# Latent attention: k-v product, turning of v and the next head's maxima one step later in the order of the queues

## Chip, cores and metric

One core of a Trainium2 chip. The metric is the device time of one execution in microseconds (us), lower is better.

## The reference, cut to what matters

The kernel computes two transformer blocks on 1024 positions. The change touches one stage of the second block, the latent attention (mla_mixer) with 12 heads. For each head:

```
q  = (rms_norm(c_q)  @ w_q_up)    # 96 columns: 64 plain, 32 turned by the positions (rope)
kv = (rms_norm(c_kv) @ w_kv_up)   # 64 columns of k, 64 of v; k gets the 32 shared rope columns
s  = q . k * 96**-0.5, causal mask; p = softmax(s); out = p @ v
```

All of it is float32 work to nearly full precision: every factor is held as a high part (fp32r) and a low part (the rest), and a product is three matmuls, high by high, high by low and low by high.

## The kernel before, in words

The five engines have queues of their own, written out as Python loops under `@block.tensor` (PE), `@block.scalar` (ACT), `@block.vector` (DVE), `@block.gpsimd` (POOL, which splits weight slabs into high and low parts) and `@block.sync` (SP, which loads them). They are held together by semaphores alone: `wait_ge` stands in the queue, and what is behind it on that engine waits too.

The latent attention runs in steps, one for each tile of transposed scores, keys by queries. A head has two chunks of 512 queries and in each the key blocks of 128 that the mask leaves: `HEAD_TILES`, 4 tiles in chunk 0 and 8 in chunk 1, so `N_HT` = 12 steps, called 0 to 11 here. The last four tiles of each chunk lie on the diagonal; they are 512, 384, 256 and 128 queries wide. For tile u:

- PE `scores(u)` (L870 the three products, L872 a fourth that subtracts each query's maximum by means of a diagonal matrix `dg`, L875 the mask on the diagonal). It goes into one of the two buffers `aux`. The first tile of chunk c waits for `dg_ready` of maximum 4c + 3, the last of its chunk.
- ACT `exponential(u)` (L1374, px) and `high_part(u)` (L1380, px_h); DVE `low_part(u)` (L1488, px_l).
- PE `values(u)` (L888, L889, L891), which stands `AV_LAG` = 2 steps later.
- Three steps after a chunk's last tile, ACT takes the logarithm of the row sums (L1391) and turns it into the inverse (L1397), around that step's `high_part`, and DVE multiplies (L1946, `weighted`).

A head needs beforehand the maxima of its queries, 8 blocks of 128: `maximum(h, i)` on PE (L852, L854) makes plain scores of block i against (i + 1) x 128 keys into the one buffer `ps[:, 0]`, DVE reduces them (L1922, which frees the buffer by `mx_free`) and writes the diagonal matrix (`diagonal`, L1929). They run `MAX_LEAD` = 5 steps ahead of the head's own steps: maxima 0 to 4 in steps 7 to 11 of the head before, 5 to 7 in steps 0 to 2.

And the next head's q, k and v are made meanwhile, in the one buffer `ps[:, 1]`: PE `latent_q` in steps 0, 1 and 2 (L811, from cq), `latent_kv` in step 4 (L811, from ckv), `latent_vt` in step 6 (the turning of v, eight transposes of kvf, L840). The ways out of the buffer stand in a table `parts` by step, behind the step's other work. ACT: 3 q without rope, 4 high part of q (qa_h), 5 the copy kvf, 6 high part of k (ka_h), 7 high part of v. DVE: 3 the rope product (L1902, qf), 5, 7 and 8 the low parts of q, k and v (L1488). `latent_kv` waits for both q parts of step 3 to have left the buffer, `latent_vt` for kvf, `maximum(h + 1, 0)` for qa_h and ka_h.

The order within a step is, on PE: scores, maximum, latent piece, values; on DVE: maximum and diagonal, low part, part, weighted; on ACT: exponential, logarithm, high part, inverse, part. The loops are quoted in the listing and the diff:

Of the kernel before, what the change touches and what calls it, by code (L numbers as in the profile page):

```python
# [35 lines left out]
MLA_HEADS = 12  # L36
# [53 lines left out]
def program(nc, wall, vecs, consts, xt, pt, memt, pos, spill_x, spill_o, spill_out, spill_gate, out):  # L90
# [240 lines left out]
             ({}, 4)  # L331
    HEAD_TILES = [(c, kb, max(kb * P - c * HALF, 0)) for c in range(2) for kb in range(4 * c + 4)]
    N_HT = len(HEAD_TILES)
    AV_LAG, MAX_LEAD = 2, 5

    def maximum_of(step):

        h, i = divmod(step + MAX_LEAD, N_HT)
        return (h, i) if i < 8 else (None, None)
# [55 lines left out]
    def _(pe):  # L395
# [34 lines left out]
        def product(ks, rh, rl, n=S, ready=None, sl=None):  # L430
            sl = slab() if sl is None else sl
            w, slot = work()
            proj(slot, sl, ks, rh, rl, n, ready)
            return w
# [37 lines left out]
        def norm_row(n):  # L472

            pe.wait_ge(rs_ready, t.next(rs_ready))
            for j in range(n // P):
                m = pe.transpose(row[:, j * P:(j + 1) * P], rs[:, j:j + 1].broadcast_to([P, P]), ident)
            m.then_inc(row_done, 1)
# [5 lines left out]
        def with_sums(make):  # L483

            for m in range(KT):
                make(m)
            tile_sums(KT, S)
# [134 lines left out]
        def from_split(ktiles):  # L622
            base = t.take(tile_split, ktiles)
            return lambda i: pe.wait_ge(tile_split, base + i + 1)
# [157 lines left out]
        def output():  # L782
            ready = from_split(KT)
            with_sums(lambda m: product(range(KT), y_h, y_l, ready=ready if m == 0 else None))
            norm_row(S)
# [32 lines left out]
        def latent_q(h, k):  # L818
            if k == 0:
                if h > 0:  # L820
                    pe.wait_ge(vl_ready, h)
                state["slab"] = slab()
            if h == 0:
                readyq(k)
            m = latent_product(state["slab"], [k], 0, 2, cq_h, cq_l, 0)
            if k == 2:
                m.then_inc(q_done, 1)

        def latent_kv(h):
            pe.wait_ge(qn_ready, h + 1)  # L830
            pe.wait_ge(rope_ready, h + 1)
            if h == 0:
                for i in range(2):
                    readykv(i)
            latent_product(state["slab"], [3, 4], 3, 4, ckv_h, ckv_l, 3).then_inc(kv_done, 1)

        def latent_vt(h):
            pe.wait_ge(kvf_ready, h + 1)
            for k in range(KT):
                m = pe.transpose(ps[:, 1, k * P:(k + 1) * P], kvf[:, k * P:(k + 1) * P], ident)  # L840
            m.then_inc(vt_done, 1)

        def maximum(h, i):

            n, keys = 8 * h + i, (i + 1) * P
            if n > 0:
                pe.wait_ge(mx_free, n)
            if i == 0:
                pe.wait_ge(qh_ready, h + 1)
                pe.wait_ge(kh_ready, h + 1)  # L850
            for a, b in widths(keys):
                pe.matmul(ps[:, 0, a:b], qa[h % 2][0][:, i * P:(i + 1) * P], ka[h % 2][0][:, a:b],  # L852
                          start=True, stop=(b < keys), skip_group_check=True)
            pe.matmul(ps[:, 0, keys - P:keys], id_r[:, :], neg_q, start=False, stop=True,  # L854
                      skip_group_check=True).then_inc(mx_done, 1)

        def scores(u):
            h, i = divmod(u, N_HT)
            c, kb, n0 = HEAD_TILES[i]
            if u >= 2:  # L860
                pe.wait_ge(ph_ready, u - 1)
            if i == 0:
                pe.wait_ge(ql_ready, h + 1)
                pe.wait_ge(kl_ready, h + 1)
            if kb == 0:
                pe.wait_ge(dg_ready, 8 * h + 4 * c + 4)
            q, k = qa[h % 2], ka[h % 2]
            st = aux[:, u % 2, n0:HALF]
            for j, (kp, qp) in enumerate(((0, 0), (0, 1), (1, 0))):
                pe.matmul(st, k[kp][:, kb * P:(kb + 1) * P], q[qp][:, c * HALF + n0:(c + 1) * HALF],  # L870
                          start=(j == 0), stop=False, skip_group_check=True)
            m = pe.matmul(st, ones_r[:, :], dg[:, c, n0:HALF], start=False, stop=(kb < 4 * c),  # L872
                          skip_group_check=True)
            if kb >= 4 * c:
                m = pe.matmul(aux[:, u % 2, n0:n0 + P], neg_q, id_r[:, :], start=False, stop=True, skip_group_check=True)  # L875
            m.then_inc(st_done, 1)

        def values(u):
            h, i = divmod(u, N_HT)
            c, kb, n0 = HEAD_TILES[i]  # L880
            g, last = 2 * h + c, kb == 4 * c + 3
            if i == 0:
                pe.wait_ge(vl_ready, h + 1)
            if kb == 0 and g >= 2:
                pe.wait_ge(ot_made, g - 1)
            pe.wait_ge(ph_ready, u + 1)
            ph, pl = px_h[u % 4][:, n0:HALF], px_l[u % 4][:, n0:HALF]
            pe.matmul(ob[:, g % 2, n0:HALF], v1[h % 2][:, kb, :], ph, start=(kb == 0), stop=False, skip_group_check=True)  # L888
            pe.matmul(ob[0:64, g % 2, n0:HALF], vl[h % 2][:, kb, :], ph, start=False, stop=False, skip_group_check=True)  # L889
            pe.wait_ge(pl_ready, u + 1)  # L890
            pe.matmul(ob[:, g % 2, n0:HALF], v1[h % 2][:, kb, :], pl, start=False, stop=last,  # L891
                      skip_group_check=True).then_inc(at_done, 1)
# [7 lines left out]
        for step in range(MLA_HEADS * N_HT + AV_LAG):  # L900
            h, i = divmod(step, N_HT)
            if h < MLA_HEADS:
                scores(step)
            mh, mi = maximum_of(step)
            if mh is not None and mh < MLA_HEADS:
                maximum(mh, mi)
            if h + 1 < MLA_HEADS:
                if i < 3:
                    latent_q(h + 1, i)
                elif i == 4:  # L910
                    latent_kv(h + 1)
                elif i == 6:
                    latent_vt(h + 1)
            if step >= AV_LAG:
                values(step - AV_LAG)
        output()


# [27 lines left out]
    def _(act):  # L946
# [417 lines left out]
            act.wait_ge(vt_done, h + 1)  # L1364
            copy(v1[h % 2][:, :, 0:64], ps[:, 1, :].rearrange("p (k f) -> p k f", k=8)[:, :, 64:P]).then_inc(vh_ready, 1)

        parts = {3: latent_q_nope, 4: latent_q_high, 5: latent_kv, 6: latent_k_high, 7: latent_v_high}

        def exponential(u):
            n0 = HEAD_TILES[u % N_HT][2]  # L1370
# [34 lines left out]
        for step in range(n_tiles + 7):  # L1405
            h, i = divmod(step, N_HT)
# [57 lines left out]
    def _(dve):  # L1464
# [137 lines left out]
        for step in range(NU + 4):  # L1602
# [12 lines left out]
            if 0 <= m < NU:  # L1615
# [4 lines left out]
                i = dve.scalar_tensor_tensor(out=e[:, :, 0:n], in0=z[:, :, 0:n], scalar=0.0, in1=e[:, :, 0:n],  # L1620
                                             op0=ALU.max, op1=ALU.add)
                if kb >= 4 * chunk:
# [3 lines left out]
                    i = dve.tensor_tensor(e[:, :, 0:c1], e[:, :, 0:c1], mask, ALU.mult)  # L1626
# [67 lines left out]
        def low_part(k):  # L1694
            dve.wait_ge(nh_ready, t.next(nh_ready))
            dve.scalar_tensor_tensor(out=hl[:, k, :], in0=x_t[:, k, :], scalar=vcol(V_MLP + k),
                                     in1=hh[:, k, :].bitcast(F32), op0=ALU.mult, op1=ALU.subtract).then_inc(norm_ready, 1)
# [216 lines left out]
            low(vl[h % 2][:, :, :], ps[:, 1, :].rearrange("p (k f) -> p k f", k=8)[:, :, 64:P],  # L1914
                v1[h % 2][:, :, 0:64]).then_inc(vl_ready, 1)

        parts = {3: latent_rope, 5: latent_q_low, 7: latent_k_low, 8: latent_v_low}

        def maximum(h, i):
            n = 8 * h + i  # L1920
            dve.wait_ge(mx_done, n + 1)
            dve.tensor_reduce(nm[:, n % 4:n % 4 + 1], ps[:, 0, 0:(i + 1) * P], AX.X, ALU.max, negate=True).then_inc(mx_free, 1)  # L1922

        def diagonal(h, i):
            n = 8 * h + i
            dve.wait_ge(mx_free, n + 1)
            if i % 4 == 0 and h > 0:
                dve.wait_ge(st_done, N_HT * h - (8 if i == 0 else 0))
            dve.tensor_scalar(dg[:, i // 4, i % 4 * P:(i % 4 + 1) * P], ident, nm[:, n % 4:n % 4 + 1],  # L1929
                              None, ALU.mult).then_inc(dg_ready, 1)  # L1930
# [24 lines left out]
        for step in range(n_tiles + AV_LAG + 2):  # L1955
            h, i = divmod(step, N_HT)
            mh, mi = maximum_of(step)
            if mh is not None and mh < MLA_HEADS:
                maximum(mh, mi)
            if mh is not None and mh < MLA_HEADS:  # L1960
                diagonal(mh, mi)
            if step < n_tiles:
                low_part(step)
            if h + 1 < MLA_HEADS and i in parts:
                parts[i](h + 1)
            done = step - AV_LAG - 1
            if done >= 0 and HEAD_TILES[done % N_HT][1] == 4 * HEAD_TILES[done % N_HT][0] + 3:
                weighted(done)
# [170 lines left out]
```

## Time and profile before

| what | before |
|---|---|
| median of 3 runs | 3587.58 us (3586.64 to 3592.84) |
| the profiled execution | 3589.34 us |
| its span | 3587.5 us |
| mean granted clock of PE over the span | 0.953 |
| busy: PE, DVE, ACT, POOL | 88%, 51%, 31%, 30% |
| latent attention in the span | about 2216 to 2568 us |

All times of rows are microseconds from the start of the span. PE stands for the matmuls, PEld for the loads of their weights beside them. Matmuls are pipelined and their ends are modelled, so a row's duration is longer than its distance to the next row. In a timeline, brackets show the idle time before a row and who ended it.

### The profile page before, as it was taken

The page shows a single profiled execution, that of the slowest core. Times are in us where ns is not written, and L with a number is a line of the kernel's source. Part 1 is how long each engine was busy: PE and PEld are TensorE (multiplying, and loading weights), DVE is VectorE, ACT ScalarE, POOL GpSimd, SP SyncE. Part 2 cuts the span into 40 slices and gives each one's busy share as a digit, 9 for nine tenths or more (in the row PEclk, how much of TensorE's full clock was granted, in tenths as well). Part 3 has the DMA queues.
Part 4 walks back from the last instruction along what each step waited for, and adds up shares of the span by engine and source line. Part 5 has one row for each costly group of instructions (what it writes and reads, how often), then busy time and mean ns, then how long its engine had stood idle before and what let it go on. Part 6 is the DMA issues. An engine that isn't in the chain of part 4 may idle for free.

```text
span 3587.5 us, 37646 instructions
## 1 busy us (share of the span) xinstructions
PE 3167.1 (88%) x15158; PEld 2616.9 (73%) x15158; DVE 1837.2 (51%) x2041; ACT 1104.9 (31%) x1682; POOL 1093.1 (30%) x426
## 2 busy tenths in 40 slices
PE   5888799999999999999787987999795789999897
PEld 4666578887788888887676776777574677777786
DVE  5788842112324334445665345777627556666543
ACT  2666720001220001001322223555523333333411
POOL 2111034444434444444245322111141211111152
PEclk9999999999899999999788998999896999999998
DMA  2000021112111111111122112000211000000131
GB/s 92 18 30 24 18 94 47 49 51 88 42 36 48 53 47 47 47 53 53 36 88 59 53 58 87 24 30 24 118 42 59 30 24 24 24 24 24 49 116 65
DMA packets 44572, 179.03 MB, mean 50 GB/s; under 512 B 4672, under 2 KB 5696, under 8 KB 43392
## 3 DMA queue, kind: packets, MB, share of 16 engines
q1 hardware_dynamic: 32976, 119.88, 11.0%
q10 hardware_dynamic: 11440, 56.89, 4.0%
q8 instruction: 120, 1.97, 0.2%
q14 instruction: 36, 0.29, 0.0%
HBM read 147.39 MB, written 29.36 MB: 49 GB/s over the span
## 4 chain that ended last, share of the span: by engine, by line
PE 75%; DVE 12%; ACT 7%; issue 4%; POOL 1%; DMA 1%; ACTq 0%; DVEq 0%; SPq 0%; POOLq 0%
PE ps L423 55%; PE ps L707 3%; PE ps L811 2%; PE ob L449 2%; PE ob L742 2%; PE aux L870 2%; PE ps L523 1%; ACT pt_h L966 1%; PE aux L725 1%; DVE pt_l L1488 1%; ACT prob L1214 1%; DVE zb L1608 1%; DVE acc L1513 1%; PE ps L852 1%; PE aux L552 1%
## 5 line engine op out<-in xcount | busy, mean ns | idle before, releaser
L380 POOL TENSOR_TENSOR wh<-raw,con 128x1024 fp32r<-128x1024 f32 x211 | 512.8, 2430 | 2433.6 <-PE ps L423 1902.7
L423 PE MATMUL ps<-hh,wh 128*128 128x512 f32 x1984 | 625.3, 397 | 39.8 <-DVE hl L1488 22.8
L423 PE MATMUL ps<-hl,wh 128*128 128x512 f32 x1984 | 619.9, 394 | 0.0
L423 PE MATMUL ps<-hh,wl 128*128 128x512 f32 x1984 | 618.4, 393 | 0.0
L382 POOL TENSOR_TENSOR wl<-raw,wh 128x1024 fp32r<-128x1024 f32 x211 | 580.2, 2750 | 16.6
L423 PEld LDWEIGHTS ps<-hh,wh 128*128 128x128 f32 x1984 | 373.6, 191 | 126.5 <-issue 36.3
L423 PEld LDWEIGHTS ps<-hl,wh 128*128 128x128 f32 x1984 | 378.5, 191 | 80.2
L423 PEld LDWEIGHTS ps<-hh,wl 128*128 128x128 f32 x1984 | 377.6, 190 | 80.2
L1730 DVE TENSOR_TENSOR y_t<-y_t,ps 128x1024 f32<-128x1024 f32 x120 | 146.5, 1221 | 174.5 <-PE ps L423 174.5
L1137 ACT ACTIVATE ff<-fr 128x1024 f32<-128x1024 f32 x32 | 34.0, 1061 | 563.7 <-DVE fr L1719 563.7
L1775 DVE TENSOR_REDUCE small<-ps 128x1 f32<-128x256 f32 (+3 forms) x160 | 105.7, 660 | 146.7 <-PE ps L707 85.1
L423 PE MATMUL ps<-f_h,wh 128*128 128x512 f32 x512 | 158.3, 390 | 2.7 <-DVE f_l L1488 2.5
L423 PE MATMUL ps<-f_h,wl 128*128 128x512 f32 x512 | 158.4, 391 | 0.0
L423 PE MATMUL ps<-f_l,wh 128*128 128x512 f32 x512 | 158.1, 390 | 0.0
L1488 DVE TENSOR_TENSOR pt_l<-aux,pt_h 128x512 fp32r<-128x512 f32 x152 | 104.4, 690 | 87.8 <-ACT pt_h L966 85.2
L1783 DVE TENSOR_SCALAR prob<-prob,small 128x256 f32<-128x256 f32 (+3 forms) x160 | 143.2, 895 | 5.7
L1513 DVE TENSOR_TENSOR acc<-acc,sq 128x1024 f32<-128x1024 f32 x40 | 80.1, 2002 | 123.9 <-ACT sq L979 123.5
L1719 DVE SCALAR_TENSOR_TENSOR fr<-ps,row_sb 128x1024 f32<-128x1024 f32 x32 | 39.2, 1224 | 192.1 <-PE ps L423 192.1
L1214 ACT ACTIVATE prob<-ps,small 128x256 f32<-128x256 f32 (+3 forms) x160 | 106.5, 665 | 46.9 <-DVE small L1775 45.7
L966 ACT ACTIVATE pt_h<-aux 128x512 fp32r<-128x512 f32 x152 | 90.3, 597 | 98.7 <-PE aux L725 97.5
L1374 ACT ACTIVATE px<-aux 128x512 f32<-128x512 f32 (+2 forms) x144 | 70.8, 492 | 155.4 <-PE aux L875 120.5
L1488 DVE TENSOR_TENSOR px_l<-px,px_h 128x512 fp32r<-128x512 f32 (+2 forms) x144 | 79.7, 553 | 71.8 <-ACT px_h L1380 71.8
(322 smaller groups left out, 5990.2 us busy)
## 6 DMA issues: line engine op xcount, KB each, us to landing
raw<-wall SPq DMA_DIRECT2D x211, 512.0 KB, 3.6
spill_x<-x_t ACTq DMA_DIRECT2D x2, 4096.0 KB, 12.1
spill_out<-ot ACTq DMA_DIRECT2D x16, 512.0 KB, 2.6
go<-spill_out ACTq DMA_DIRECT2D x16, 512.0 KB, 4.3
xold_t<-spill_x ACTq DMA_DIRECT2D x2, 4096.0 KB, 15.5
x_t<-xt SPq DMA_DIRECT2D x8, 512.0 KB, 8.9
spill_o<-op ACTq DMA_DIRECT2D x4, 1024.0 KB, 3.9
o_all<-spill_o ACTq DMA_DIRECT2D x2, 2048.0 KB, 10.3
```

Of the source, the lines that this page charges most:

```text
L380: pool.tensor_tensor(wh[:, s, :, :], raw[:, s, :, :], ones.unsqueeze(1).broadcast_to([P, KT, P]), ALU.mult).then_inc(w_high, 1)
L382: pool.tensor_tensor(wl[:, s, :, :], raw[:, s, :, :], wh[:, s, :, :].bitcast(F32), ALU.subtract).then_inc(w_split, 1)
L423: m = pe.matmul(ps[:, w, a:b], lw[:, sl, k, :], r[:, i, a:b], start=(i == 0 and j == 0), stop=(i == len(ks) - 1 and j == 2))
L449: m = pe.matmul(ob[:, bank, j:j + 1], src[:, j * P:(j + 1) * P], ones[:, 0:1], start=False, stop=True, skip_group_check=True)
L707: m = pe.matmul(ps[:, slot, a:b], l, r[0:n_rows, a:b], start=(j == 0), stop=(j == len(parts) - 1 and not masked), skip_group_check=True)
L966: return act.activation(out_, in_, ACT.Copy, scale=scale)
L1214: act.activation(prob[now % 2][i][:, 0:keys], ps[:, w % 2, 0:keys], ACT.Exp, bias=nm[:, j:j + 1], scale=1.0, accum_out=rsum[:, j:j + 1]).t ...
L1488: return dve.tensor_tensor(dst, src, hi.bitcast(F32), ALU.subtract)
L1513: dve.tensor_tensor(acc[:, :], acc[:, :], sq[(first + k) % 2][:, :], ALU.add).then_inc(sq_used, 1)
L1730: dve.tensor_tensor(y_t[:, m, :], y_t[:, m, :], ps[:, slot, :], ALU.add).then_inc(work_free[slot], 1)
L1775: dve.tensor_reduce(nm[:, i:i + 1], ps[:, slot, 0:keys_of(n % 4)], AX.X, ALU.max, negate=True).then_inc(nm_ready, 1)
L1783: dve.tensor_scalar(p, p, rinv[:, i:i + 1], None, ALU.mult).then_inc(pn_ready, 1)
```

## The change

The lead of the maxima falls from 5 steps to 4: maxima 0 to 3 in steps 8 to 11, 4 to 7 in steps 0 to 3. On PE the k-v product moves from step 4 to 5 and the turning of v from 6 to 7; maximum 0 stands behind the values of its step. On ACT the parts of k and v (kvf, ka_h, high part of v) each move one step, on DVE the low parts of k and v; there maximum 0 and its diagonal stand behind the low part of the step. The q parts stay.

```
--- before.py
+++ after.py
@@ -331,7 +331,7 @@
              ({}, 4)
     HEAD_TILES = [(c, kb, max(kb * P - c * HALF, 0)) for c in range(2) for kb in range(4 * c + 4)]
     N_HT = len(HEAD_TILES)
-    AV_LAG, MAX_LEAD = 2, 5
+    AV_LAG, MAX_LEAD = 2, 4
 
     def maximum_of(step):
 
@@ -902,17 +902,20 @@
             if h < MLA_HEADS:
                 scores(step)
             mh, mi = maximum_of(step)
-            if mh is not None and mh < MLA_HEADS:
+            due = mh is not None and mh < MLA_HEADS
+            if due and mi > 0:
                 maximum(mh, mi)
             if h + 1 < MLA_HEADS:
                 if i < 3:
                     latent_q(h + 1, i)
-                elif i == 4:
+                elif i == 5:
                     latent_kv(h + 1)
-                elif i == 6:
+                elif i == 7:
                     latent_vt(h + 1)
             if step >= AV_LAG:
                 values(step - AV_LAG)
+            if due and mi == 0:
+                maximum(mh, mi)
         output()
 
 
@@ -1364,7 +1367,7 @@
             act.wait_ge(vt_done, h + 1)
             copy(v1[h % 2][:, :, 0:64], ps[:, 1, :].rearrange("p (k f) -> p k f", k=8)[:, :, 64:P]).then_inc(vh_ready, 1)
 
-        parts = {3: latent_q_nope, 4: latent_q_high, 5: latent_kv, 6: latent_k_high, 7: latent_v_high}
+        parts = {3: latent_q_nope, 4: latent_q_high, 6: latent_kv, 7: latent_k_high, 8: latent_v_high}
 
         def exponential(u):
             n0 = HEAD_TILES[u % N_HT][2]
@@ -1914,7 +1917,7 @@
             low(vl[h % 2][:, :, :], ps[:, 1, :].rearrange("p (k f) -> p k f", k=8)[:, :, 64:P],
                 v1[h % 2][:, :, 0:64]).then_inc(vl_ready, 1)
 
-        parts = {3: latent_rope, 5: latent_q_low, 7: latent_k_low, 8: latent_v_low}
+        parts = {3: latent_rope, 5: latent_q_low, 8: latent_k_low, 9: latent_v_low}
 
         def maximum(h, i):
             n = 8 * h + i
@@ -1955,12 +1958,15 @@
         for step in range(n_tiles + AV_LAG + 2):
             h, i = divmod(step, N_HT)
             mh, mi = maximum_of(step)
-            if mh is not None and mh < MLA_HEADS:
+            due = mh is not None and mh < MLA_HEADS
+            if due and mi > 0:
                 maximum(mh, mi)
-            if mh is not None and mh < MLA_HEADS:
                 diagonal(mh, mi)
             if step < n_tiles:
                 low_part(step)
+            if due and mi == 0:
+                maximum(mh, mi)
+                diagonal(mh, mi)
             if h + 1 < MLA_HEADS and i in parts:
                 parts[i](h + 1)
             done = step - AV_LAG - 1
```

## Rows read from the trace of the kernel before

**Rows 1.** Busy time in two stretches: stick-breaking stage, ten heads of latent attention. Columns: first line.

```profile
core 0: us, PE busy (x) PEld busy (x) DVE busy (x) ACT busy (x) POOL busy (x), PEclk, DMA share, GB/s
80.00:470.00 390.00, 316.74 (x1445) 243.49 (x1444) 311.77 (x331) 258.14 (x319) 47.73 (x18) 0.95 0.07 22
2228.32:2529.03 300.71, 277.48 (x1500) 229.91 (x1501) 218.94 (x340) 170.91 (x331) 52.64 (x20) 1.00 0.08 25
```

**Rows 2.** The waits between 2228 and 2559 us: us in total, times, longest.

```profile
PE ps L840 <- ACT kvf L966: 9.8, 11, 0.9
PE ps L811 <- DVE qf L1902: 7.9, 11, 0.7
PE ps L852 <- ACT ka_h L966: 7.6, 11, 0.8
```

**Rows 3.** Timeline of PE over one head: start, duration, operation, idle before.

```profile
2324.78 1.09 PE L840 MATMUL ps<-con,kvf 128*128 128x128 f32 x8 [0.90 <-ACT kvf L966]
2325.63 0.48 PE L888 MATMUL ob<-px_h,v_b 128*128 128x512 f32 x1
...
2326.88 0.39 PE L870 MATMUL aux<-qa_h,ka_l 128*128 128x512 f32 x1
2327.10 0.40 PE L872 MATMUL aux<-dg,ones_r 128*128 128x512 f32 x1
2328.34 0.30 PE L852 MATMUL ps<-ka_h,qa_h 128*128 128x128 f32 x1 [0.84 <-ACT ka_h L966]
...
2328.59 0.44 PE L888 MATMUL ob<-px_h,v_b 128*128 128x512 f32 x1
...
2330.32 0.33 PE L852 MATMUL ps<-ka_h,qa_h 128*128 128x256 f32 x1
...
2335.24 0.51 PE L852 MATMUL ps<-ka_h,qa_h 128*128 128x512 f32 x2
...
2335.69 0.39 PE L888 MATMUL ob<-px_h,v_b 128*128 128x384 f32 x1
...
2336.26 0.40 PE L870 MATMUL aux<-qa_h,ka_h 128*128 128x512 f32 x1
...
2348.63 0.70 PE L811 MATMUL ps<-ckv_h,wh 128*128 128x512 f32 x2 [0.72 <-DVE qf L1902]
```

**Rows 4.** Timelines of PE, then DVE, in the last head, from maximum 7.

```profile
2551.17 0.73 PE L852 MATMUL ps<-ka_h,qa_h 128*128 128x512 f32 x2 [0.31 <-DVE small L1922]
...
2551.79 0.45 PE L888 MATMUL ob<-px_h,v_b 128*128 128x512 f32 x1
...
2553.68 0.47 PE L870 MATMUL aux<-qa_h,ka_h 128*128 128x512 f32 x1
...
2553.25 0.29 DVE L1929 TENSOR_SCALAR dg<-con,small 128x128 fp32r<-128x128 f32 x1
```

**Rows 5.** Timeline of ACT over the same head, steps 5, 6 and 8.

```profile
2323.70 1.03 ACT L966 ACTIVATE kvf<-ps 128x1024 f32<-128x1024 f32 x1
2324.61 0.62 ACT L1374 ACTIVATE px<-aux 128x512 f32<-128x512 f32 x1
...
2327.14 1.06 ACT L966 ACTIVATE ka_h<-kvf 64x1024 fp32r<-64x1024 f32 x1
...
2330.51 0.60 ACT L1374 ACTIVATE px<-aux 128x512 f32<-128x512 f32 x1 [0.87 <-PE aux L875]
2331.01 0.59 ACT L1380 ACTIVATE px_h<-aux 128x512 fp32r<-128x512 f32 x1
```

**Rows 6.** Timeline of DVE over the same head, reduction 0 to diagonal 3.

```profile
2328.79 0.29 DVE L1922 TENSOR_REDUCE small<-ps 128x1 f32<-128x128 f32 x1 [0.88 <-PE ps L854]
...
2329.32 0.69 DVE L1488 TENSOR_TENSOR px_l<-px,px_h 128x512 fp32r<-128x512 f32 x1
2329.92 1.21 DVE L1488 TENSOR_TENSOR ka_l<-kvf,ka_h 64x1024 fp32r<-64x1024 f32 x1
...
2334.90 0.29 DVE L1929 TENSOR_SCALAR dg<-con,small 128x128 fp32r<-128x128 f32 x1
2335.10 0.42 DVE L1488 TENSOR_TENSOR px_l<-px,px_h 128x256 fp32r<-128x256 f32 x1
```

More of the change, by code:

```diff
@@ L333, in program @@
     N_HT = len(HEAD_TILES)
-    AV_LAG, MAX_LEAD = 2, 5
+    AV_LAG, MAX_LEAD = 2, 4
     def maximum_of(step):
@@ L904, in _ @@
             mh, mi = maximum_of(step)
-            if mh is not None and mh < MLA_HEADS:
+            due = mh is not None and mh < MLA_HEADS
+            if due and mi > 0:
                 maximum(mh, mi)
@@ L909, in _ @@
                     latent_q(h + 1, i)
-                elif i == 4:
+                elif i == 5:
                     latent_kv(h + 1)
-                elif i == 6:
+                elif i == 7:
                     latent_vt(h + 1)
@@ L915, in _ @@
                 values(step - AV_LAG)
+            if due and mi == 0:
+                maximum(mh, mi)
         output()
@@ L1365, in latent_v_high @@
             copy(v1[h % 2][:, :, 0:64], ps[:, 1, :].rearrange("p (k f) -> p k f", k=8)[:, :, 64:P]).then_inc(vh_ready, 1)
-        parts = {3: latent_q_nope, 4: latent_q_high, 5: latent_kv, 6: latent_k_high, 7: latent_v_high}
+        parts = {3: latent_q_nope, 4: latent_q_high, 6: latent_kv, 7: latent_k_high, 8: latent_v_high}
         def exponential(u):
@@ L1915, in latent_v_low @@
                 v1[h % 2][:, :, 0:64]).then_inc(vl_ready, 1)
-        parts = {3: latent_rope, 5: latent_q_low, 7: latent_k_low, 8: latent_v_low}
+        parts = {3: latent_rope, 5: latent_q_low, 8: latent_k_low, 9: latent_v_low}
         def maximum(h, i):
@@ L1957, in _ @@
             mh, mi = maximum_of(step)
-            if mh is not None and mh < MLA_HEADS:
+            due = mh is not None and mh < MLA_HEADS
+            if due and mi > 0:
                 maximum(mh, mi)
-            if mh is not None and mh < MLA_HEADS:
                 diagonal(mh, mi)
@@ L1963, in _ @@
                 low_part(step)
+            if due and mi == 0:
+                maximum(mh, mi)
+                diagonal(mh, mi)
             if h + 1 < MLA_HEADS and i in parts:
```

## Prediction

> **What bounds the kernel now.** I read the page for the shares, then the busy time by stretches, then the waits of the stage that the diff touches, and last the timelines of PE, ACT and DVE over one head. In the ten full heads of the latent attention, 2228.32 to 2529.03 us, the granted clock is 1.00, the level of 2.4 GHz, and PE is busy 277.48 of 300.71 us, 27.8 of 30.07 per head; the other engines have room [rows 1]. So the stage goes by PE's own queue, and what can be won or lost is PE's standing still. The reader should look in the waits for lines that name PE: only three come once per head, 11 times each, for the k-v product (ps<-ckv, L811, waits for qf), the turning of v (L840, waits for kvf) and the next head's first maximum (L852, waits for ka_h) [rows 2]. The change moves just these three.
>
> I number the steps 0 to 11 within a head. A 512-column matmul of the scores is shown 0.40 long, while the next starts 0.23 after it, at 2327.10 behind 2326.88 [rows 3]. A shown idle time must therefore be enlarged by about 0.16 to get the time in which PE issued nothing. The three waits are then 0.72 + 0.16 = 0.88, 0.90 + 0.16 = 1.06 and 0.84 + 0.16 = 1.00, together **2.94 us per head** [rows 3]; all three gone would be 32 us.
>
> **The change part by part.** No instruction and no DMA is added or removed; the order in the queues of PE, ACT and DVE is. SP and POOL keep their code: the weight slab of the next head is asked for by the same q product in step 0. What POOL does to DVE's diagonals while it splits the slab now falls on maxima 4 and 5, not 5 and 6; only the low parts of steps 0 and 1 stand behind them, and PE wants those two steps later. I cost it at nothing.
>
> *k-v product, step 4 to 5.* It waits for the q copy on ACT and the rope product on DVE, both of part 3. It gets the PE work of scores 5 and values 2 in between, over a microsecond, and the wait of 0.88 goes. Late next are the scores of step 4 themselves (next point).
>
> *Maxima 1 to 7, one step later.* The last maximum (1024 keys) was in step 2, a whole step ahead of the scores of step 4, which need its diagonal (dg_ready). It now stands in step 3, with only values 1 behind it. The last head shows the round trip without other work: the maximum's matmuls start at 2551.17, the scores of step 4 at 2553.68, so 2.51 us through the reduction, the diagonal and back [rows 4]. PE's own work in that time will be the maximum (2551.17 to 2551.79, 0.62) and values 1 (0.57, as for the 384 columns of values 9, 2335.69 to 2336.26 [rows 3]). **New wait at scores 4: 2.51 - 0.62 - 0.57 = 1.32 us.** Bounds 1.1 and 1.5. Rope now stands behind that last reduction on DVE (and behind the low part of step 3), but it ends before PE is through scores 4, values 2 and scores 5.
>
> *Turning of v, step 6 to 7.* It needs the copy kvf on ACT, which moves from ACT's step 5 to step 6. There ACT's queue holds the two exponentials of the tile and, because chunk 0 ended three steps before, the logarithm and the inverse of its sums, all ahead of the moved part. Before, ka_h stood in that place: from px at 2324.61 to ka_h at 2327.14 are 2.53 us [rows 5]. kvf now starts 2.53 us after px of step 6, lasts 1.03, and the turning follows 0.05 later (2323.70 + 1.03 against 2324.78) [rows 3, 5]. px starts 0.19 after PE has issued its scores (2330.32 and 2330.51) [rows 3, 5]. PE covers values 4 and scores 7, 2325.63 to 2327.10 and 0.23 more, 1.70 us [rows 3]. **Wait at the turning: 0.19 + 2.53 + 1.03 + 0.05 - 1.70 = 2.10 us**, in place of 1.06. In the heads where ACT's pair is a little shorter it is 0.25 less, and so was the old wait for ka_h; the balance is the same. Bounds 1.8 and 2.4.
>
> *First maximum, step 7 to the end of step 8.* It needs ka_h, which ACT now makes in step 7, right behind kvf and two exponentials; meanwhile PE turns v and does values 5, scores 8 and values 6, some 3 us. The old wait of 1.00 goes. But on DVE its reduction now stands behind low part 8, which waits for px_h of the same step, and all maxima share one buffer, so each waits for the reduction before (mx_free). DVE has been nearly without a gap from reduction 0 to diagonal 3: 2328.79 to 2334.90 + 0.29, 6.40 us [rows 6]. That chain keeps k_low, v_low, the four reductions and diagonals, loses low parts 7 and 8 (0.60 each, 2329.32 to 2329.92) and takes low part 10 (0.42 long, some 0.35 in sequence) in place of nothing: 6.40 - 1.20 + 0.35 = 5.55 us [rows 6]. It starts, counted from the end of scores 8 on PE, after 0.19 to px, 0.50 to px_h, 0.59 of px_h, 0.04, and low part 8 (0.60): 1.92 [rows 5, 6]. The last diagonal ends at 7.47, and the next head's scores 0, which need it, start 0.14 later (as from 2553.25 + 0.29 to 2553.68): 7.61 [rows 4]. PE's own work in that time was 2330.32 to 2336.26, 5.94; it loses maximum 4 (2335.24 to 2335.69, 0.45) and gets maximum 0 (0.25, 2328.34 to 2328.59): 5.74 [rows 3]. **Waits of maxima 1 to 3 and of scores 0 together: 7.61 - 5.74 = 1.87 us per head.** By my split they are 0.5, 0.3, 0.3 and 0.8. Bounds 0.9 (only the wait of scores 0, which no order of the low parts hides) and 2.5 (each handover dearer by 0.15).
>
> *Ends of the stage.* In the last head no q product parts the maxima 4 to 7, and DVE is already late there (0.31 idle before the last maximum [rows 4]); I take 1.9 us for it, between 1.3 (the wait of scores 4 alone) and 2.5. Before the first head one maximum of 640 keys leaves the serial prologue: 0.45 at full clock [rows 3], twice that at the half level; I take -0.5, between 0 and -1.0.
>
> **Sum.** Per head 1.32 + 2.10 + 1.87 - 2.94 = +2.35 us, over 11 heads +25.9; with +1.9 and -0.5 it is **+27.3 us**. The profiled execution took 3589.34 us with a span of 3587.5, the median is 3587.58; I put the sum on the median: **3614.9 us**, 0.76% slower. What a measurement of this kernel can tell from no change is about 0.2%, 7 us.
>
> **Rivals.** *DVE keeps pace.* If the waits of 1.87 did not arise, because DVE's chain packs more tightly than its rows show, +0.48 per head remains: 5.3 + 1.3 - 0.5 = +6 us, 3593.7, just inside no change. For it: the six rows of the chain are read out of a queue that was itself waiting now and then. Against it: the reduction of maximum 0 comes behind low part 8 by the code, and scores 0 need a diagonal whose maximum stands one short values group ahead. Chance 0.08.
>
> *The clock falls.* PE's busy share would go from 0.92 to about 0.86. The stick-breaking stage from 80 to 470 us shows 316.74 of 390, 0.81, at a mean granted clock of 0.95, while this stage has 1.00 [rows 1]. If this stage fell to 0.95 as well, part of it at 1.2 instead of 2.4 GHz, its PE work of some 333 us (12 heads of 27.8 at most) would take 18 us more: +45, 3633. Against it: the longest new pause is 2 us, and the work round it is dense. Chance 0.04. The Trainium skill (TensorE: Matmul & The Clock Gate, section "HAM oscillation — how this bites in real kernels") tells of this mechanism: pauses between bursts of matmuls that throw the clock back to half again and again. By that rule the added pauses could cost more than their own length; the trace of before, with three pauses a head, shows no fall.
>
> *Faster.* The three old waits are real and each moved part has a step more. If kvf came through ACT ahead of the logarithm and the inverse, and DVE gave its diagonals in time, only the turning's wait would stay: -(0.88 + 1.00) x 11 = -21 us, 3567. The place is ACT's step 6, and the point is whether kvf starts within 1.49 us of px: then the turning waits 0.19 + 1.49 + 1.03 + 0.05 - 1.70 = 1.06, no longer than before. 2.53 us of work stand ahead of it in a queue that goes in order. Chance 0.03. That the change leaves the order as it was is ruled out by the code; that gains and losses cancel otherwise has 0.01.
>
> **How the numbers follow.** Forecast 0.84, DVE keeps pace 0.08, clock 0.04, faster 0.03, cancelled 0.01. With all terms at their low bounds a head costs 1.1 + 1.8 + 0.9 - 2.94 = +0.9, in all about +10; at their high ones 1.5 + 2.4 + 2.5 - 2.94 = +3.5, in all +40. These do not come all together, so the range is 3601 to 3627 us. Slower by over 0.2%: forecast, clock and a quarter of the second case, 0.90. Within 0.2%: 0.07. Faster: 0.03.
>
> **What would show it.** In the changed profile PE should be idle before L870 at step 4 with DVE small or dg named (about 1.2), before L840 with kvf (near 1.9), no longer before L811 and no longer for ka_h before L852; before L852 of maxima 1 to 3 some tenths for DVE small, before L870 of step 0 about 0.7. The head's period should go from 30.1 to 32.4 us. A period at or under 30.1, a wait at L840 of 1 us or less, or a granted clock under 1.00 would prove me wrong.

## The result, and the profile after

| what | before | after |
|---|---|---|
| median | 3590.21 us of 4 runs (3586.64 to 3594.32) | 3621.13 us of 4 runs (3618.60 to 3624.94) |
| ratio, with its 95% interval | | 1.0087 [1.0069, 1.0104] |
| span of the profiled execution | 3587.5 us | 3621.2 us |
| a head of the latent attention, mean of ten | 30.07 us | 32.54 us |

The change makes the kernel slower by 0.87%, 31 us by the medians of the same round; the forecast was 27 us and 0.76%. The same work is done: 37646 instructions in both. Busy times by stretch for ten heads, from k-v product to k-v product (columns: window, its length, then the busy time of each engine, the granted clock, DMA):

```profile
core 0: us, PE busy (x) PEld busy (x) DVE busy (x) ACT busy (x) POOL busy (x), PEclk, DMA share, GB/s
2233.41:2558.77 325.36, 283.55 (x1502) 231.97 (x1501) 222.08 (x340) 171.44 (x331) 52.65 (x20) 1.00 0.08 23
```

Against [rows 1], ten heads take 325.36 us in place of 300.71, with the same number of DVE and ACT instructions (340, 331) and the same granted clock of 1.00. PE's busy time is 6 us larger although it does the same work: the modelled end of a matmul covers the first 0.16 us of every pause, and there are now six pauses a head instead of three, which makes 4.8 of the 6 us. So the loss is standing time on PE. The waits of the stage name it (us in total, times, longest):

```profile
PEld ps L840 <- ACT kvf L969: 25.2, 11, 2.4
...
PE aux L870 <- DVE dg L1932: 20.9, 23, 1.4
PE ps L840 <- ACT kvf L969: 20.6, 11, 2.0
...
PE ps L852 <- DVE small L1925: 4.4, 12, 0.4
```

Compare [rows 2]. The waits of L811 for qf and of L852 for ka_h, 7.9 and 7.6 us, are gone. L840's wait for kvf is doubled, from 9.8 to 20.6, and L870's wait for a diagonal is new, 20.9 us in 23 pieces: twice in each of eleven heads (scores 4, and scores 0 of the next head), once in the last. The timeline of PE over one head shows where (it answers to [rows 3]):

```profile
2361.28 0.47 PE L870 MATMUL aux<-qa_h,ka_h 128*128 128x512 f32 x1 [1.15 <-DVE dg L1932]
...
2363.56 0.62 PE L811 MATMUL ps<-ckv_h,wh 128*128 128x512 f32 x2
...
2368.88 0.39 PE L872 MATMUL aux<-dg,ones_r 128*128 128x512 f32 x1
2371.01 1.09 PE L840 MATMUL ps<-con,kvf 128*128 128x128 f32 x8 [1.74 <-ACT kvf L969]
...
2375.89 0.39 PE L852 MATMUL ps<-ka_h,qa_h 128*128 128x256 f32 x1 [0.37 <-DVE small L1925]
...
2377.40 0.22 PE L875 MATMUL aux<-id_r,neg_r 128*128 128x128 f32 x1
2377.68 0.44 PE L852 MATMUL ps<-ka_h,qa_h 128*128 128x384 f32 x1
...
2379.15 0.27 PE L875 MATMUL aux<-id_r,neg_r 128*128 128x128 f32 x1
2379.53 0.50 PE L852 MATMUL ps<-ka_h,qa_h 128*128 128x512 f32 x1
...
2381.28 0.47 PE L870 MATMUL aux<-qa_h,ka_h 128*128 128x512 f32 x1 [0.62 <-DVE dg L1932]
...
2393.69 0.47 PE L870 MATMUL aux<-qa_h,ka_h 128*128 128x512 f32 x1 [1.15 <-DVE dg L1932]
```

The first row is the scores of step 4, the last row those of the next head. The pauses, with the modelled tails (0.16 to 0.17) added to what the brackets show, are 1.32 at scores 4, none at the k-v product, 1.90 at the turning, 0.53, 0.22 and 0.32 at maxima 1, 2 and 3, and 0.78 at scores 0. The short ones at maxima 2 and 3 carry no bracket, since the tail of the matmul before covers them: they are read off as 2377.40 + 0.06 against 2377.68 and 2379.15 + 0.06 against 2379.53. The heads come in two kinds that take turns, even and odd numbers from 0: this one is even (number 4), the head read before the change in [rows 3] is odd (number 3). In the odd heads the turning waits 2.18.

And the timeline of ACT in steps 6 and 7 of this head (it answers to [rows 5]):

```profile
2367.70 0.60 ACT L1377 ACTIVATE px<-aux 128x512 f32<-128x512 f32 x1 [2.08 <-PE aux L872]
2368.32 0.60 ACT L1394 ACTIVATE inv<-ob 64x512 f32<-64x512 f32 x1
2368.95 0.60 ACT L1383 ACTIVATE px_h<-aux 128x512 fp32r<-128x512 f32 x1
2369.44 0.62 ACT L1400 ACTIVATE inv<-inv 64x512 f32<-64x512 f32 x1
2369.96 1.00 ACT L969 ACTIVATE kvf<-ps 128x1024 f32<-128x1024 f32 x1
```

ACT stands idle for 2.08 us, although the k-v product it has to copy was there by 2366.5, because its queue wants the scores of step 6 first; then four softmax operations precede the copy. From px to kvf are 2.26 us here; in the odd head that follows they are 2.52 (2400.09 to 2402.61), which is the difference in the turning's wait. Why the two kinds differ was not looked into.

The timeline of DVE from low part 8 on (it answers to [rows 6]):

```profile
2374.95 0.69 DVE L1491 TENSOR_TENSOR px_l<-px,px_h 128x512 fp32r<-128x512 f32 x1 [2.30 <-ACT px_h L1383]
2375.56 0.28 DVE L1925 TENSOR_REDUCE small<-ps 128x1 f32<-128x128 f32 x1
...
2376.08 1.21 DVE L1491 TENSOR_TENSOR ka_l<-kvf,ka_h 64x1024 fp32r<-64x1024 f32 x1
...
2378.32 0.68 DVE L1491 TENSOR_TENSOR vl_b<-ps,v_b 128x512 fp32r<-128x512 f32 x1
...
2380.12 0.69 DVE L1925 TENSOR_REDUCE small<-ps 128x1 f32<-128x512 f32 x1
2380.85 0.29 DVE L1932 TENSOR_SCALAR dg<-con,small 128x128 fp32r<-128x128 f32 x1
```

From reduction 0 to the end of diagonal 3 DVE is never idle for 5.58 us, and the scores that need the diagonal start 0.14 later, at 2381.28.

### The profile page after: what moved, and what is told of

Read it like the earlier page. It is cut to its first block, busy times and chain, and to the rows that moved or that the text cites. A ratio compares the mean times of both kernels' runs of the same rounds, so it can differ in the third digit from the quotient of the medians.

```text
span 3621.2 us, 37646 instructions
## 1 busy us (share of the span) xinstructions
PE 3188.7 (88%) x15158; PEld 2631.3 (73%) x15158; DVE 1841.2 (51%) x2041; ACT 1105.1 (31%) x1682; POOL 1093.4 (30%) x426
## 4 chain that ended last, share of the span: by engine, by line
PE 74%; DVE 14%; ACT 7%; issue 4%; POOL 1%; DMA 1%; ACTq 0%; DVEq 0%; SPq 0%; POOLq 0%
PE ps L423 54%; PE ps L707 3%; PE ps L811 2%; PE ob L449 2%; PE aux L870 2%; PE ob L742 2%; ACT pt_h L969 1%; PE aux L725 1%; PE ps L523 1%; DVE pt_l L1491 1%; ACT prob L1217 1%; DVE small L1925 1%; PE aux L552 1%; DVE zb L1611 1%; DVE acc L1516 1%
## 5 line engine op out<-in xcount | busy, mean ns | idle before, releaser
L1140 ACT ACTIVATE ff<-fr 128x1024 f32<-128x1024 f32 x32 | 33.9, 1061 | 563.7 <-DVE fr L1722 563.7
```

## The experiments

Each kernel was timed against the kernel before. "Head" is the mean distance of the k-v products over ten heads of its profile, "stage" the time from the first scores to the last values product, which is free of what the rest of the program does from run to run (the part ahead of the stage alone differed by 3.2 us between the first two profiles).

| kernel | ratio to before [95%] | head, us | stage, us |
|---|---|---|---|
| before | 1 | 30.07 | 350.78 |
| the change | 1.0087 [1.0069, 1.0104] | 32.54 | 380.05 |
| e1, lead alone | 1.0057 [1.0040, 1.0074] | 31.70 | 372.47 |
| e2, pieces alone | 1.0019 [1.0008, 1.0030] | 30.69 | 357.18 |
| e3, change, copy first on ACT | 1.0020 [1.0009, 1.0032] | 30.65 | 359.24 |
| e4, change, maximum 7 first | 1.0080 [1.0063, 1.0097] | 32.56 | 379.77 |
| e5, change, low part of v later | 1.0070 [1.0051, 1.0088] | 32.40 | 378.46 |
| e6, the three waits gone | 0.9917 [0.9903, 0.9931] | 27.44 | 321.98 |
| e8, e6 with DVE as before | 0.9941 [0.9925, 0.9958] | 28.51 | 333.62 |
| e9, e6 with lead 4 | 0.9990 [0.9980, 0.9999] | 29.53 | 348.75 |

**Lead alone.** The kernel before, with

```
-    AV_LAG, MAX_LEAD = 2, 5
+    AV_LAG, MAX_LEAD = 2, 4
```

> The maxima alone one step later (lead 4), k-v product and turning as before. Theory (each wait is the chain on DVE or ACT less PE's cover): scores of step 4 wait 1.32 us for the last diagonal; the k-v product, still in step 4, waits some 0.5 for rope, which now stands behind that reduction; the turning 1.06 as before; the first maximum no more; scores 0 some 0.8. In all 3.7 against 2.94 us a head, so 11 x 0.8, plus 1.9 in the last head, less 0.6 before the first: about +10 us against before, head period 30.9. Rival (the whole loss of the change is the shorter lead of the maxima, and the moved pieces are a gain by themselves): +31 us or more.

It came out twice as dear, +20 us of the medians and +21.7 in the stage. The waits in two heads of the profile: 1.32 at scores 4, 0.46 at the k-v product, 1.06 at the turning and 0.79 at scores 0, all as expected, and besides 0.53 or 0.26 at maximum 1 and 0.29 at maximum 2, which I had put at nothing. DVE's timeline shows why:

```profile
2339.14 1.21 DVE L1488 TENSOR_TENSOR ka_l<-kvf,ka_h 64x1024 fp32r<-64x1024 f32 x1
2340.28 0.28 DVE L1922 TENSOR_REDUCE small<-ps 128x1 f32<-128x128 f32 x1
2340.59 0.29 DVE L1929 TENSOR_SCALAR dg<-con,small 128x128 fp32r<-128x128 f32 x1
2340.79 0.68 DVE L1488 TENSOR_TENSOR px_l<-px,px_h 128x512 fp32r<-128x512 f32 x1
2341.39 0.69 DVE L1488 TENSOR_TENSOR vl_a<-ps,v_a 128x512 fp32r<-128x512 f32 x1
2341.99 0.42 DVE L1922 TENSOR_REDUCE small<-ps 128x1 f32<-128x256 f32 x1
```

The low part of k (step 7) stands ahead of reduction 0, that of v (step 8) ahead of reduction 1, and PE needs the single maxima buffer back sooner than they let DVE come to it. I had also taken 2.94 us a head as the old wait; the mean of both kinds of head is 2.81. And some 1.5 us of the 21.7 are no price of the lead: the last head took 22.8 us against 21.3 in the changed kernel, since PE's clock fell behind the pause before scores 4. The first row below is the matmul that ends the pause, the second the stretch behind it (columns as in [rows 1], granted clock 0.50):

```profile
2576.62 0.51 PE L870 MATMUL aux<-qa_h,ka_h 128*128 128x512 f32 x1 [1.44 <-DVE dg L1929]
2576.90:2580.30 3.40, 3.40 (x11) 2.79 (x10) 0.69 (x1) 1.09 (x2) 0.00 (x0) 0.50 0.00 0
```

The rival, that the lead is the whole loss, falls: it is two thirds of it.

**Pieces alone.** The changed kernel, with

```
-    AV_LAG, MAX_LEAD = 2, 4
+    AV_LAG, MAX_LEAD = 2, 5
```

> The k-v product, the turning of v and their ways out one step later, maximum 0 last in its step 7, but the lead of the maxima stays 5. Theory: no wait at the k-v product and none of scores 4 or scores 0 for a diagonal; the turning waits 1.9 for kvf as in the changed kernel, since the copy stands behind the logarithm and the inverse on ACT; maximum 0 waits 0.4 for ka_h, maxima 3 and 4 about 0.4 each for DVE. Some 3.1 against 2.94 us a head: +2 us against before (between -3 and +8). Rival (moved pieces are a gain): the turning waits 1.06 or less and the kernel is 10 to 21 us faster than before.

+6.2 us by the medians, +6.4 in the stage. The turning waits 1.90 or 2.18, maximum 0 0.37 or 0.53, maxima 3 and 4 0.36 and 0.39; the rival is refuted. Two of ten heads took 31.7 us instead of 30.7, since PE's clock fell behind the pause at the turning. In one of them the pause lasted until 2331.31 (busy times of three stretches, the granted clock is the third figure from the end):

```profile
2325.00:2331.30 6.30, 4.29 (x21) 3.18 (x19) 3.21 (x4) 3.98 (x8) 0.00 (x0) 1.00 0.00 0
2331.30:2335.50 4.20, 4.19 (x17) 3.67 (x18) 1.27 (x3) 1.99 (x3) 0.00 (x0) 0.59 0.00 0
2335.50:2340.00 4.50, 4.31 (x26) 3.72 (x25) 3.60 (x7) 3.11 (x7) 0.00 (x0) 1.00 0.00 0
```

Most of that middle stretch was granted 1.2 GHz, the rest 2.4. Of the 0.62 us that a head costs more than before, these two falls make 0.2 in the mean of ten, and the waits the rest.

**Copy first.** The changed kernel, on ACT (the part of step 6 is left out of the table's call):

```
             done = step - AV_LAG - 1
+            if i == 6 and h + 1 < MLA_HEADS:
+                latent_kv(h + 1)
             if step < n_tiles:
                 exponential(step)
```

> The changed kernel with one thing moved: on ACT the copy kvf comes first in step 6, ahead of the exponential, where ACT stands idle for 2.1 us. Theory (the turning's wait of 1.90 is the order of ACT's queue): the wait at L840 is gone, the other waits stay, -1.9 x 11 = -21 us against the changed kernel, +10 against before, head period 30.5. Rival (ACT as a whole is late, or the waits merely move on to DVE's chain, which must run anyway): less than 5 us are won and the waits of maxima 1 to 3 and of scores 0 grow by what the turning loses.

23 us below the changed kernel by the two medians (25 if each is taken against the kernel before of its own rounds), 20.8 in the stage, as the theory said (21). ACT's and PE's timelines of one head:

```profile
2362.03 1.03 ACT L969 ACTIVATE kvf<-ps 128x1024 f32<-128x1024 f32 x1 [0.88 <-PE ps L811]
2363.24 0.60 ACT L1377 ACTIVATE px<-aux 128x512 f32<-128x512 f32 x1 [0.19 <-PE aux L872]
```

```profile
2364.43 0.39 PE L872 MATMUL aux<-dg,ones_r 128*128 128x512 f32 x1
2364.66 1.03 PE L840 MATMUL ps<-con,kvf 128*128 128x128 f32 x8
```

The copy fits into ACT's idle time and is over before the scores of step 6 are; the turning follows the scores of step 7 without a bracket. The other waits stayed (1.32, 0.53 or 0.73, 0.22, 0.32, 0.79). So the turning's wait was the order of ACT's queue: with one copy moved it is gone, and of the other waits only those of maxima 0 and 1 grew, by 0.14 and 0.2 in every other head.

**Maximum 7 first.** The changed kernel, on PE:

```
+            if due and mi == 7:
+                maximum(mh, mi)
             if h < MLA_HEADS:
                 scores(step)
-            if due and mi > 0:
+            if due and 0 < mi < 7:
                 maximum(mh, mi)
```

> The changed kernel with one thing moved on PE: maximum 7 stands ahead of the scores of step 3 instead of behind them. Theory (the wait of scores 4, 1.32 us, is the fixed way through reduction and diagonal less the work that PE has in between): 0.50 us of scores are added to the cover, the wait falls to 0.8 in the full heads, less in the last one where DVE is late; -5 to -6 us against the changed kernel, +25 against before. Rival (the wait ends when DVE is through its queue, however early the maximum comes): the wait stays 1.3 and the time too.

The time as a whole did not move by more than its noise, but the head did, in both directions. Where nothing else happened it took 31.86 and 32.29 us, against 32.40 and 32.67: the wait of scores 4 fell from 1.32 to 0.95, not quite to 0.82. DVE's timeline has the missing 0.13:

```profile
2350.81 1.95 DVE L1934 TENSOR_SCALAR dg<-con,small 128x128 fp32r<-128x128 f32 x1
...
2354.26 1.44 DVE L1934 TENSOR_SCALAR dg<-con,small 128x128 fp32r<-128x128 f32 x1
...
2357.86 0.69 DVE L1951 TENSOR_TENSOR ot<-ob,inv 64x512 f32<-64x512 f32 x1
2358.57 1.23 DVE L1927 TENSOR_REDUCE small<-ps 128x1 f32<-128x1024 f32 x1
```

DVE is never idle from diagonal 4 to reduction 7, which starts 0.44 us behind the maximum's last matmul (2358.13), where in the changed kernel it starts 0.26 behind it (0.05 of the 0.18 comes back, since the maximum's own matmuls are shorter by that). Two diagonals in that chain, 4 and 5, took 1.95 and 1.44 us instead of 0.29; they lie beside POOL's splitting of the next weight slab (2350.28 to 2355.62). Three heads took 33.9 us, each with its clock falling behind the turning's pause, 1.6 us more than its like: 4.9 us, as much as the shorter wait wins (11 times some 0.45). For the wait the theory holds for 0.37 us of the 0.50, and the rival, DVE's queue, for the rest; the total is inconclusive.

**Low part of v later.** The changed kernel, on DVE:

```
-        parts = {3: latent_rope, 5: latent_q_low, 8: latent_k_low, 9: latent_v_low}
+        parts = {3: latent_rope, 5: latent_q_low, 8: latent_k_low, 11: latent_v_low}
```

> The changed kernel with the low part of v moved on DVE from step 9 to step 11, behind the last diagonal that scores 0 need. Theory (the waits of maxima 1 to 3 and of scores 0, 1.85 us together, are one chain on DVE that has no gap): the chain is 0.60 us shorter and so are the waits, to 1.25; -6.6 us against the changed kernel, +25 against before. Rival (each of these waits is the latency of one handover between PE and DVE, whatever else DVE does): they stay 0.5, 0.2, 0.3 and 0.8 and the time stays.

Half of what the theory said: a head of 32.11 or 32.38 us, 0.3 less, with one head of 34.0 where the clock fell (the medians, 3618.88 against 3621.13, are too close to tell). The wait of maximum 3 is gone, those of maxima 1 and 2 stay (DVE's work ahead of them is the same), and that of scores 0 stays at 0.78. DVE's timeline tells why the last did not follow:

```profile
2383.24 0.42 DVE L1491 TENSOR_TENSOR px_l<-px,px_h 128x256 fp32r<-128x256 f32 x1
2383.93 0.69 DVE L1925 TENSOR_REDUCE small<-ps 128x1 f32<-128x512 f32 x1 [0.27 <-PE ps L854]
2384.66 0.29 DVE L1932 TENSOR_SCALAR dg<-con,small 128x128 fp32r<-128x128 f32 x1
```

Once DVE is early enough, reduction 3 waits for PE's maximum, and the way from there through reduction, diagonal and back is fixed. In the changed kernel both limits lay in the same place: there reduction 3 starts at 2380.12, without a bracket, right behind the low part of its step.

**The three waits gone.** The kernel before, with the k-v product in step 5 on PE, and

```
# ACT
+            ahead = i == 6 and h + 1 < MLA_HEADS
+            if ahead:
+                latent_kv(h + 1)
             if step < n_tiles:
                 exponential(step)
+            if ahead:
+                latent_k_high(h + 1)
...
# DVE
-        parts = {3: latent_rope, 5: latent_q_low, 7: latent_k_low, 8: latent_v_low}
+        parts = {3: latent_rope, 5: latent_q_low, 10: latent_v_low}
...
+            if i == 6 and h + 1 < MLA_HEADS:
+                latent_k_low(h + 1)
             if step < n_tiles:
                 low_part(step)
```

> The kernel before, with the k-v product in step 5, the turning still in step 6, the lead still 5; on ACT kvf first in step 6 and ka_h right behind that step's first exponential; on DVE the low part of k ahead of low part 6 and the low part of v in step 10. Theory (the three waits of before, 2.94 us a head by the one head read and some 2.8 in the mean, are orders of queues and not work): they fall to some 0.1 to 0.4 a head, -27 to -31 us against before, head period 27.4, about 3560 us. Rival (DVE's chain of reductions, diagonals and low parts is the bound behind them, 6.4 us without a gap): the waits come back at L852 for DVE small, and less than 15 us are won.

3561.30 us against 3591.96, 30.7 us faster than before, ratio 0.9917 [0.9903, 0.9931], a head of 27.44 us. The rows show first two waits of DVE and ACT that cost nothing, since both have idle time there, and then all that is left of PE's waits for other engines from the first k-v product on; by the distances of the starts, 0.17 or 0.29 us a head is left at maximum 1 besides:

```profile
DVE ka_l L1493 <- ACT ka_h L966: 20.5, 11, 1.9
ACT kvf L966 <- PE ps L811: 10.3, 11, 1.0
...
PEld ps L852 <- DVE small L1927: 4.0, 12, 0.5
PEld ps L840 <- ACT kvf L966: 3.7, 11, 0.3
...
PE ps L852 <- DVE small L1927: 0.3, 1, 0.3
```

It is the best version of the study. The first half of the change, one step more for the k-v product, is in it; the turning of v, the maxima and their lead are where they were.

**With DVE as before.** e6, with the low part of k back in DVE's step 7 and that of v in step 8.

> The kernel in which the three waits were gone (e6), but with DVE's order as in the kernel before: low part of k in step 7, of v in step 8. Theory: with PE's waits gone DVE's chain becomes the bound where the low parts stand between the reductions: maxima 2 and 3 wait some 0.7 and 0.4 us, head period 28.5, +12 us against e6 and -18 against before. Rival (DVE had room, the moves on PE and ACT alone made the gain): no wait at L852 beyond 0.3, as fast as e6, -30 against before.

A head of 28.51 us and 11.6 us more than e6 in the stage, as expected (28.5 and 12). Once a head, 11 times each, these stand in PE's timeline, at maxima 2 and 3 (0.58 and 0.37 with the tails, 0.7 and 0.4 expected):

```profile
2327.60 0.44 PE L852 MATMUL ps<-ka_h,qa_h 128*128 128x384 f32 x1 [0.42 <-DVE small L1927]
...
2329.59 0.50 PE L852 MATMUL ps<-ka_h,qa_h 128*128 128x512 f32 x1 [0.21 <-DVE small L1927]
```

**Lead 4 on the best.** e6, with MAX_LEAD 4 and nothing else.

> The kernel in which the three waits were gone (e6) with the lead of the maxima 4 instead of 5 and nothing else. Theory (the shorter lead has a price of its own, independent of the old waits): scores 4 wait 1.3 and scores 0 some 0.8 to 1.0, the maxima 1 to 3 hardly; 2.1 to 2.4 us a head and 2.0 in the last, +25 to +28 us against e6, so -3 to -6 against before. Rival (the shorter lead costs only together with the late k and v): within 5 us of e6.

A head of 29.53 us, 2.09 more than e6, and 26.8 us more in the stage, of which 1.5 are a fall of the clock in the last head, as in e1; 3.5 us below before by the medians. Only the two waits for diagonals are left, and they are whole:

```profile
2363.41 0.47 PE L870 MATMUL aux<-qa_h,ka_h 128*128 128x512 f32 x1 [0.75 <-DVE dg L1934]
```

and the one of 1.15 at scores 4 as in the changed kernel. So the shorter lead has a price of its own, with k and v ready in good time.

## Why the prediction was right, point by point

- *Sum.* +27.3 us was forecast; the medians say +30.9 (interval +25 to +37). In the two profiles the prologue of the stage got 0.62 shorter (-0.5 forecast), the eleven head periods from scores 0 to scores 0 took 27.3 more (25.9), the last head 1.96 more (1.9): 28.6 for all three. The other 5 us by which the spans differ lie before and behind, where the code is the same. 3621.13 is in the range, and the mechanism held on which the main chance rested: each wait is a chain on ACT or DVE less the work that PE has meanwhile.
- *Scores 4.* Forecast 1.32 from the last head's round trip less PE's cover; measured 1.32 in every head but the last. e4 and e9 show it with other neighbours.
- *Turning.* Forecast 2.10 by an odd head; measured 2.18 in the odd heads and 1.90 in the even ones. The forecast called the other kind 0.25 less, so that step was right; e3 confirms the cause by taking it away.
- *k-v product and first maximum.* Both old waits vanished, as forecast.
- *Maxima 1 to 3 and scores 0.* Forecast 1.87, measured 1.85 (0.53, 0.22, 0.32, 0.78). The chain on DVE was forecast at 5.55 us and took 5.58. The size was right and its reason half right: I derived the whole from that gapless chain, but e5 shows that the last 0.78 is also the plain round trip of the last maximum, so that a shorter chain wins only 0.3. The forecast's lower bound of 0.9, "only the wait of scores 0, which no order of the low parts hides", had said so; the expectation of e5 forgot it.
- *Where the remaining 1.4 us of the head periods come from.* Per head +2.35 was forecast; the odd heads took 2.45 more than before and the even ones 2.47 to 2.49. The old waits of 2.94 were those of an odd head (the mean of both kinds is 2.81), but so was the turning's 2.10, and the two nearly cancel: with measured waits the balance is 1.32 + 2.03 + 1.85 - 2.81 = 2.39. The other 0.08 a head stand in no wait that was read, and stay open. The first head took 2.66 more: its first steps run at the half clock, and 0.2 us longer so than before the change.
- *POOL beside the diagonals.* Costed at nothing, and rightly here: diagonals 4 and 5 take some 1.9 to 2.0 and 1.44 us instead of 0.29, but DVE is idle again for 0.41 us before the reduction of maximum 7 (2359.58), so no matmul waited for them. In e4, where that maximum came earlier, they were part of what it waited for.
- *Rivals.* "DVE keeps pace" and "faster" did not come; the point named for the latter, whether kvf starts within 1.49 us of px, came out at 2.52 in the odd heads (2.53 was read) and 2.26 in the even ones, and when e3 put it ahead of px the wait was gone. "The clock falls" did not happen in the profile of the changed kernel, whose clock is 1.00 over all ten heads; it did happen in single heads of e1, e2, e4, e5 and e9 (last section), so the rival had more ground than the forecast gave it, at 1.0 to 1.6 us a fall and not at 18 us.

What the forecast did not draw from its own rows is that this stage holds a gain nearer than the change: it named 32 us as what the three waits are worth, and e6 brings 28.8 of it in the stage (30.7 by the medians), by one step's delay of the k-v product and the order of ACT's and DVE's queues.

## What to carry to other kernels

Moving a piece one step later helps only if what it waits for does not become late as well. So read what stands ahead of the producer in the producer's own queue at its new place, and how much work the engine that sets the pace has in the meantime. A round trip (here maximum, reduction, diagonal, scores: 2.5 us) needs a whole step of other work to hide behind, and its length can be read from any place of the old trace where nothing else fills it. If an engine stands idle just ahead of the copy that others wait for, move the copy to the front of its step, before touching the bound engine's schedule.

## What the runs showed of the hardware that I had not expected

PE's clock fell to its half level behind single pauses in an otherwise dense stretch (the busy times of e2 and e1 above). In the profiles of the change, e2, e4 and e5 the turning's pause is shown as 2.02 us in the odd heads and 1.74 in the even ones; the clock fell behind 6 of the 20 longer ones (none in the change, 2 in e2, 3 in e4, 1 in e5) and behind none of the 24 shorter ones. But a still shorter pause did it too: before scores 4 of the last head five profiles show 1.43 or 1.44 us, and the clock fell behind it in e1 and e9, and not in the change, e3 and e5. So the length of the pause alone does not decide; what does was not tried. In the kernel before, e6 and e8, whose longest pause in the ten full heads is shown as 0.90 us, there was no fall. A fall cost 1.0 us in e2, some 1.6 in e4 and e5, and some 1.5 in e1 and e9. The rule of the Trainium skill that the forecast weighed (TensorE: Matmul & The Clock Gate, "HAM oscillation — how this bites in real kernels") has its trace here in these eight heads, at a small price. The pauses of that section's example are longer, about 3 to 5 us; the measurement here says that shorter ones can do it.
